# Turning three more hidden tiles per FFN layer by DMA, and moving one tile's copies in step 10

## The reference, cut to what matters

```python
def swiglu(h, w_gu, w_down):
    gu = h @ w_gu
    g, u = gu[..., :D_FF], gu[..., D_FF:]
    return (jax.nn.silu(g) * u) @ w_down

for i in range(DEPTH):                      # DEPTH = 2, D_FF = 2816
    ...
    h = h + rmsnorm(m, norm_mix_post[i])
    f = swiglu(rmsnorm(h, norm_ffn_pre[i]), ffn_w_gu[i], ffn_w_down[i])
    h = h + rmsnorm(f, norm_ffn_post[i])
```

## Time and profile before

| | us |
|---|---|
| median of 3 runs | 814.19 (814.08 to 814.84) |
| the profiled execution | 814.93 |
| its span, first to last instruction | 812.9 |
| TensorE busy in the span | 801.4 |
| VectorE busy | 511.5 |
| ScalarE busy | 455.5 |
| GpSimd busy | 96.7 |
| granted clock of TensorE, mean | 0.998 of full speed |

### The profile page before, as it was taken

One profiled execution on the slowest core, in us unless ns is written; L12 is line 12 of the kernel. 1 busy time (PEld: TensorE's weight loads), 2 busy tenths in 40 slices (PEclk: granted clock), 3 DMA queues, 4 the chain that ended last, 5 costly groups with the idle time before them and its releaser, 6 DMA issues.

```text
span 812.9 us, 11748 instructions
## 1 busy us (share of the span) xinstructions
PE 801.4 (99%) x4377; PEld 643.5 (79%) x4377; DVE 511.5 (63%) x1073; ACT 455.5 (56%) x879; POOL 96.7 (12%) x159
## 2 busy tenths in 40 slices
PE   9999999999999999999999999999999999999996
PEld 7877675788888888788877878878877888888885
DVE  5966979786646464686565665666568765555444
ACT  7836878764535353575555666555558553535331
POOL 1000005700222222000000000000000012222210
PEclk9999999999999999999999999999999999999999
DMA  9955211166986687558444535363434667767711
GB/s 318 346 186 197 88 54 53 63 223 195 234 216 191 191 244 216 170 194 273 153 160 145 167 115 197 104 206 105 156 110 142 196 226 203 207 184 238 224 32 52
DMA packets 126312, 141.69 MB, mean 174 GB/s; under 512 B 23680, under 2 KB 109744, under 8 KB 126128
## 3 DMA queue, kind: packets, MB, share of 16 engines
q1 hardware_dynamic: 125168, 136.73, 54.6%
q0 software_dynamic: 992, 4.19, 1.3%
q10 hardware_dynamic: 96, 0.02, 0.0%
HBM read 134.64 MB, written 2.10 MB: 168 GB/s over the span
## 4 chain that ended last, share of the span: by engine, by line
PE 83%; DMA 6%; issue 4%; POOL 3%; DVE 2%; ACT 1%; POOLq 0%; ACTq 0%; DVEq 0%
PE ps L1785 73%; PE ps L1794 6%; DMA planes_t<-planes 6%; POOL ht L684 2%; PE ps L2062 2%; PE ps L2035 2%; POOL planes L679 1%; PE ps L1847 1%; PE ps L2073 1%; ACT junk L740 0%; ACT xd_hi L728 0%; DVE w_lo L1231 0%; DVE h L1555 0%; DVE h L1561 0%; DVE tmp L1559 0%
## 5 line engine op out<-in xcount | busy, mean ns | idle before, releaser
L1231 DVE TENSOR_TENSOR w_lo<-w_raw,w_hi 128x1024 fp32r<-128x1024 f32 x240 | 288.5, 1229 | 73.3 <-ACT w_hi L719 71.0
L719 ACT ACTIVATE w_hi<-w_raw 128x1024 fp32r<-128x1024 f32 x240 | 246.1, 1061 | 2.9 <-DMA w_raw<-in_ffn_w_gu 2.7
L1785 PE MATMUL ps<-w_hi,xt_hi 128*128 128x512 f32 x472 | 188.8, 401 | 0.0
L1785 PE MATMUL ps<-w_hi,xt_lo 128*128 128x512 f32 x472 | 183.6, 390 | 0.0
L1785 PE MATMUL ps<-w_lo,xt_hi 128*128 128x512 f32 x472 | 183.0, 390 | 0.0
L1785 PE MATMUL ps<-w_hi,xd_hi 128*128 128x512 f32 x288 | 117.4, 408 | 0.2 <-DVE w_lo L1231 0.2
L1785 PE MATMUL ps<-w_hi,xd_lo 128*128 128x512 f32 x288 | 113.2, 393 | 0.0
L1785 PE MATMUL ps<-w_lo,xd_hi 128*128 128x512 f32 x288 | 112.8, 392 | 0.0
L1785 PEld LDWEIGHTS ps<-w_hi,xt_hi 128*128 128x128 f32 x472 | 88.5, 188 | 24.5 <-issue 8.2
L986 ACT ACTIVATE silu<-ps,rs 128x256 f32<-128x256 f32 x44 | 20.9, 474 | 151.2 <-PE ps L1785 151.1
L1785 PEld LDWEIGHTS ps<-w_hi,xt_lo 128*128 128x128 f32 x472 | 88.6, 188 | 18.8
(11 more groups left out here) (259 smaller groups left out, 936.0 us busy)
## 6 DMA issues: line engine op xcount, KB each, us to landing
w_raw<-in_ffn_w_gu SPq DMA_DIRECT2D x88, 512.0 KB, 5.1
w_raw<-in_dil_w_in SPq DMA_DIRECT2D x72, 512.0 KB, 4.6
w_raw<-in_ffn_w_down SPq DMA_DIRECT2D x44, 512.0 KB, 4.9
w_raw<-in_nsa_w_in SPq DMA_DIRECT2D x20, 512.0 KB, 7.3
w_raw<-in_nsa_w_o SPq DMA_DIRECT2D x8, 512.0 KB, 4.7
w_raw<-in_dil_w_o SPq DMA_DIRECT2D x8, 512.0 KB, 4.4
w_k<-in_nsa_cmp_wk SPq DMA_DIRECT2D x2, 1024.0 KB, 9.1
w_raw<-in_nsa_cmp_wv SPq DMA_DIRECT2D x2, 1024.0 KB, 11.6
```

The lines of the kernel that those rows point to most:

```text
L719: act.activation(w_hi[:, n.slot, c:c + 1024], w_raw[:, n.slot, c:c + 1024], ACT.Copy)\
L1231: dve.tensor_tensor(w_lo[:, n.slot, c:c + 1024], w_raw[:, n.slot, c:c + 1024], w_hi[:, n.slot, c:c + 1024].bitcast(F32), ALU.subtract)\
L1785: ins = pe.matmul(o, s, m, start=start, stop=stop, **kw)
```

## The change

Three more tiles in each layer, (0,0), (1,0) and (1,1), are turned over GpSimd and DMA. `XBAR` becomes a list of tiles. TensorE keeps the turns of (0,1), (10,0) and (10,1). GpSimd splits tile (0,0) before it issues the gain's broadcast, and merges it after that. SP's transposes of the three tiles stand in front of the loads of pieces n0+7, n0+9 and n0+11. On ScalarE and VectorE the split of n0+6 goes in front of ht_out(1,0). In step 10, ht_out(9,1) goes behind silu(10,0) on ScalarE and behind hs(10,0) on VectorE, and there also behind the second half of the split of the next piece.

```diff
-XBAR = range(2, FJ - 1)
+XBAR = [(0, 0), (1, 0), (1, 1)] + [(j, m) for j in range(2, FJ - 1) for m in range(MT)]
 def xbar_no(layer, j, m):
-    return MT * (len(XBAR) * layer + j - XBAR[0]) + m
+    return len(XBAR) * layer + XBAR.index((j, m))
+def xbar_of(layer, j, m):
+    tiles = [x for x in XBAR if x[1] == m]
+    return len(tiles) * layer + tiles.index((j, m)) + 1
...
             def turns_before(n):                                       # SP
-                    for j in XBAR:
-                        if n == first + 3 * j + 6:
-                            turn_planes(layer, j, 0)
-                        if n == first + 3 * j + 8:
-                            turn_planes(layer, j, 1)
+                    for j, m in XBAR:
+                        if n == first + max(3 * j + 6 + 2 * m, RING):
+                            turn_planes(layer, j, m)
...
+            def split_hidden(layer, j, m):                             # GpSimd
+                pool.wait_ge(hs_ready, ffn_order(layer, j, m) + 1)
+                pool.tensor_copy(view(planes, ...), halves_of(hs[:, m, :])).then_inc(planes_ready, 1)
+            def merge_hidden(layer, j, m):
+                pool.wait_ge(planes_turned[m], 16 * xbar_of(layer, j, m))
+                if (j - 2, m) in XBAR:
+                    pool.wait_ge(ht_ready, ffn_order(layer, j - 2, m) + 1)
+                pool.tensor_copy(halves_of(ht[:, j % 2, m, :]), view(planes_t, ...)).then_inc(ht_merged, 1)
             def turn_hidden(layer):
+                merge_hidden(layer, *XBAR[0])
+                for j, m in XBAR[1:]:
+                    split_hidden(layer, j, m)
+                    merge_hidden(layer, j, m)
             for b in range(1, 4):
+                if b != 2:
+                    split_hidden(b // 2, *XBAR[0])
                 pool.wait_ge(h_ready[b][1], MT)
                 if b != 2:
                     post_gain(b + 1, *nexts[b])
...
                 def ht_out(j, m):                                      # ScalarE
+                    if (j, m) in XBAR:
                         act.wait_ge(ht_merged, xbar_no(layer, j, m) + 1)
+                        if j:
+                            act.wait_ge(*((piece_used, n0 + 3 * j + 2) if m else (down_first, (FJ - 1) * layer + j)))
...
                 silu_step(0, 1)                                        # ScalarE; VectorE alike with hs_step
+                split(Piece(n0 + 6))
                 ht_out(1, 0)
-                split(Piece(n0 + 6))
                 ht_out(0, 1)
...
                 split(nx)                                              # step 10; VectorE alike with hs_step
-                ht_out(j - 1, 1)
                 split(nx + 1, (0,))
                 silu_step(j, 0)
                 split(nx + 1, (1,))
+                ht_out(j - 1, 1)
                 ht_out(j, 0)
...
-                    gu(j, 1, pc, mid=(lambda: ht_turn(1, 1)) if j == 2 else None)      # TensorE
+                    gu(j, 1, pc)
...
                 gu(1, 0, Piece(n0 + 2), mid=turn_h)
-                pe.wait_ge(xt_ready[b], 3)
-                ht_turn(0, 0)
+                pe.wait_ge(hs_ready, ffn_order(layer, 0, 0) + 1)
                 gu(0, 1, Piece(n0), need=need(1))
                 down(0, 0, Piece(n0 + 4), first=True)
-                ht_turn(1, 0)
+                pe.wait_ge(hs_ready, ffn_order(layer, 1, 0) + 1)
                 gu(1, 1, Piece(n0 + 2), mid=lambda: ht_turn(0, 1))
```

More of the change, by code:

```diff
@@ L345, in turn_no @@
         def turn_no(layer, j, m):
-            return 6 * layer + (2 * m + j if j < 2 else 4 + m)
+            return 3 * layer + (0 if j == 0 else 1 + m)
         def ffn_order(layer, j, m):
@@ L358, in ht_from @@
         def ht_from(j, m):
-            if j in XBAR:
+            if (j, m) in XBAR:
                 return ht[:, j % 2, m, :].rearrange("p (a t) -> p a t", a=2)
@@ L671, in halves_of @@
                 return t.bitcast(U16).rearrange("p (i k) -> p k i", k=2)
-            def turn_hidden(layer):
[L675 to L685, removed]
+            def split_hidden(layer, j, m):
+                pool.wait_ge(hs_ready, ffn_order(layer, j, m) + 1)
+                pool.tensor_copy(view(planes, (j % 2 * MT + m) * 512, [[256, 2], [1, 256]]), halves_of(hs[:, m, :]))\
+                    .then_inc(planes_ready, 1)
+            def merge_hidden(layer, j, m):
+                pool.wait_ge(planes_turned[m], 16 * xbar_of(layer, j, m))
+                if (j - 2, m) in XBAR:
+                    pool.wait_ge(ht_ready, ffn_order(layer, j - 2, m) + 1)
+                pool.tensor_copy(halves_of(ht[:, j % 2, m, :]),
+                                 view(planes_t, (j % 2 * MT + m) * 512, [[256, 2], [1, 256]])).then_inc(ht_merged, 1)
+            def turn_hidden(layer):
+                merge_hidden(layer, *XBAR[0])
+                for j, m in XBAR[1:]:
+                    split_hidden(layer, j, m)
+                    merge_hidden(layer, j, m)
             for b in range(1, 4):
+                if b != 2:
+                    split_hidden(b // 2, *XBAR[0])
                 pool.wait_ge(h_ready[b][1], MT)
@@ L1565, in hs_step @@
                 def hs_step(j, m):
-                    if j - 1 in XBAR:
+                    if (j - 1, m) in XBAR:
                         dve.wait_ge(planes_ready, xbar_no(layer, j - 1, m) + 1)
```

## The result

The changed kernel took 820.06 us (median of 6 runs, 819.16 to 821.87), the kernel before 814.36 (6 runs, 814.08 to 816.12): ratio 1.0068, 95% interval 1.0055 to 1.0082. Forecast was 813.8, with 812.0 to 816.2 as the range; the time lies outside. The profiled execution took 819.71 us, span 817.0. It is one of the three of the six executions with a mean granted clock of 0.995 or 0.996, which took 819.16 to 819.78 us; the other three, at 0.993, took 820.33 to 821.87, and what cost them the difference no trace shows.

A forecast was written before the change was run, and what follows sets the result against it. TensorE, 99% busy, was taken to bound the kernel. Gains 1.56 + 1.06, less stalls 0.85 and 0.4 and twice 0.5 for the broadcast, made 0.37 us faster: 813.8 us for the median, range 812.0 to 816.2.

The forecast's parts named there:

- A turn: On TensorE, one tile's turn was put at 0.26 us; six removed over both layers gain 1.56 us.
- Step 10: Layer 0, moving ht_out(9,1) later lets down(10,0) start at 328.3 instead of 329.34: 1.06 us gained; layer 1 nothing.
- wait of down(10,0): Step 10 of layer 0: down(10,0) was to wait about 0.6 us for end_lo.
- GpSimd's copy of (1,0) and the half-splits of n0+4 do collide: Beside GpSimd's copy (1.68 us), VectorE's pair of half-splits takes 2.77 instead of 2.35 us: 0.41 more.
- The chain to the stall: Tile (0,0) by DMA delays the n0+4 split; down(0,0) stalls 0.85 us in layer 0, no stall or slack in layer 1.
- c: What the gain's broadcast adds to the transpose of (0,0): 0.5 us taken per layer, between 0 and 1.8.
- rival 3: Broadcast goes wholly before the first transpose, adding 1.8 us in both layers: 2.2 us slower, 816.4; chance 0.13.
- (1,0): Its DMA transpose, behind the load of n0+8, stalls down(0,1) by 0 to 0.75 us per layer; 0.2 taken.
- T: Start of the first matmul of down(0,0), which releases the load of n0+8; (1,0)'s merge was put at T + 6.0.

The follow-up runs named there:

- run 8: Changed kernel with tiles (0,0) and (1,0) left on TensorE, only (1,1) turned by DMA: 813.14 us, ratio 0.9977 to the kernel before.
- run 5: Changed kernel with VectorE's split of n0+4 before ht_out(0,0) and SP's transpose of (1,0) before the load of n0+8: 812.49 us, ratio 0.9970.
- run 2: Kernel before with only the step 10 part, ht_out(9,1) moved behind silu(10,0), hs(10,0) and the half-split that follows: 813.45 us, ratio 0.9981.
- run 10: The changed kernel itself measured once more, with its own profile, for the clock: 820.26 us, ratio 1.0066 to the kernel before.
- run 1: Changed kernel with the gain's broadcast issued only after GpSimd's merge of tile (0,0): 815.8 us, ratio 1.0012 to the kernel before.
- run 9: Changed kernel with the gain's broadcast in two halves of 256 KB, the second after the merge of (0,0): 818.84 us, ratio 1.0052.
- run 4: Changed kernel with VectorE's split of piece n0+4 moved in front of ht_out(0,0): 814.73 us, ratio 0.9994 to the kernel before.
- run 3: Changed kernel with 16 unused identity transposes added on TensorE before down(0,0) in both layers: 819.61 us, ratio 1.0052 to the kernel before.
- run 6: Changed kernel with the split first, (1,0)'s transpose before the load, and the gain's broadcast after the merge of (0,0): 812.11 us, ratio 0.9966.
- run 7: Changed kernel with tile (0,0) left on TensorE, only (1,0) and (1,1) turned by DMA: 814.45 us, ratio 0.9997 to the kernel before.

## Why the prediction was wrong

**Right, and shown.** A turn costs 0.26 us (run 8: 0.26 and 0.25; run 5: 0.71 and 0.81 for three). Step 10 gains 1.06 (0.97 in the profile after, 1.0 in run 2), with a wait of down(10,0) of 0.46 where 0.6 was said. GpSimd's copy of (1,0) and the half-splits of n0+4 do collide: 1.54 and 2.76, against 1.68 and 2.77. The chain to the stall holds too: down(0,0) starts 2.89 us behind its slot in layer 0 (179.11 against 177.06 - 0.26 - 0.58, which this execution was ahead by) and 2.19 in layer 1 (645.20 against 640.98 - 0.26 + 2.29, as this FFN began 2.29 later than before), where 0.85 + 1.83 = 2.68 and 0.01 + 1.99 = 2.00 follow from the prediction's working with c as measured.

**The step that failed first: c.** I took 0.5 and gave the bound of 1.8, rival 3, a chance of 0.13. The reasons, that "by the rows the transpose's data starts first" and that "of the transpose's 0.75 us only the last 0.35 meet the bulk", set the transpose's first data (1.2 us after its issue) against the broadcast's bulk (1.65 after). By their first packets the two were alike in the kernel before: the broadcast's moved at 169.6, 1.25 us after its issue, the transpose's of tile (2,0) at 197.0, 1.22 after. In the change the broadcast is issued 0.09 us ahead, and most of its data ran in front: the transpose's first packet moved 2.7 us after its issue. Measured 1.83 and 1.99 instead of twice 0.5: 2.8 us, and as both layers were without slack, all of it is stall. Rival 3 had named this mechanism, and the sign; its 816.4 is short of the rest. By the Trainium skill, DMA: Bandwidth & Descriptors, section Queues, rings and completion order, with its turns packet by packet, c would have been 0.75 (an estimate), and about the same for half the broadcast; the runs have 1.83 to 1.99 and 1.33. Its sign was right, the measurement decides the size, and this trace has no such turns before 172.4 us. Why the transpose's packets stood back no row shows.

**A term that was missing: the clock.** The sum charged a stall its length. Behind the 2.72 us in layer 0 the clock was at 1.2 GHz for most of nine matmuls: from 179.11 to 182.74 are 3.63 us, where nine take 2.04 at full clock, so 1.6 us. With 2.89 of stall and three turns of 0.26 won that makes 3.71 of the 3.83 lost there. Run 10 shows it again; waits of 2.05 to 2.24 us in four places (layer 1 of the changed kernel and of run 10, runs 1 and 9) had no fall behind them in the profiles. With c at 0.5 the stall would have been 1.35, shorter than all of these, so by them the clock would not have fallen (argued, not run): the error of one term brought in the second.

**A term that was too small: (1,0).** I took 0.2 in each layer, bound 0.75, from a merge at T + 6.0 and at most T + 6.9. It came at T + 6.3 to T + 8.85 in the runs that left it behind the load. In the changed kernel it shows little (653.95, some 0.2 late, in layer 1), because in layer 0 the slow matmuls give it 1.6 us. Alone it is the 1.39 and 0.58 of run 4. The price of the clock is therefore not 1.6 net. In run 4, down(0,1) starts 2.05 us after the merge (183.92 to 185.97), and its slot is T + 8.42; so with merges at T + 6.95 (the profile) and T + 7.98 (run 10) it would have waited about 0.6 and 1.6 us at full clock. That is an estimate. Run 3, at full clock, agrees: merge at T + 8.19, down(0,1) 2.05 behind it, so 1.82 late, 1.52 of it idle.

**The sum again, as measured:** 1.56 and 0.97 gained, 2.89 + 2.19 stall, 1.6 clock, about 0.3 for (1,0): 4.45 lost, of the 4.7 in the profile. The medians are 5.7 apart (820.06 - 814.36); what the other 1.0 us is, the two traces do not show.

**What was not seen.** The prediction named what is queued behind the tile on VectorE, the half-splits of n0+4, and took that as given. Run 4 shows that this was the whole price of c, since those half-splits need nothing of the tile, and run 6 that behind this order c is worth nothing. And it named the load in front of (1,0)'s transpose; run 5 shows that moving it behind the transpose costs nothing.

## What to carry to other kernels

When a short chain through DMA replaces work on the engine, look first at what is queued behind its end on each engine and on the issuing queue: independent work goes in front of the wait, and the small urgent transfer in front of the large one that is not urgent; here these two moves turned 0.68% slower into 0.30% faster. Where a term lies between far bounds and the place has no slack, give its bad bound a real chance: a broadcast issued within 0.1 us of an urgent transfer moved most of its data first here. Compare first packets with first packets, not with the other's bulk. Before two losses in one stage are added, ask whether the first gives the second its time: the slow clock covered the late tile of layer 0, and taking it away alone (run 3) won only 0.16%, less than the runs can tell apart.

## What the hardware showed that was not expected

- A transpose of 128 KB beside a broadcast of 512 KB from another queue: 4.41 to 4.76 us from issue to merge, in both layers of the changed kernel and runs 3, 4, 5 and 10, instead of 2.51 to 2.68 alone (runs 1 and 6); beside 256 KB, 3.91 and 3.90. In layer 0 its first packet moved 2.7 us after its issue (256 KB: 2.0) instead of 1.25, behind 111 of the broadcast's 144.
- A transpose behind a 1 MB load on its own queue: 4.86 to 7.37 us from issue to merge in the changed kernel and runs 1, 3, 4, 7, 9 and 10 (6.54 in layer 0 of run 4); 3.80 and 3.13 when issued ahead of the load (run 5).
- TensorE's granted clock fell to 1.2 GHz after waits of 2.72 and 2.84 us, for 3 us or so, and not after waits of 0.90 to 2.24 us in these profiles, nor after the 1.46 of the kernel before.
- A wait costs TensorE some 0.3 us more than the idle time that its timeline shows (run 7: 1.02 for 0.68 and 0.75 for 0.47).
